# A two-block network on one core: the first inverse level, a value tile, a table product and a norm's order are moved, and unread products are added

## The reference, cut to what matters

```python
def stick_breaking_attention(u, w_q, k, v, w_o):
    q = (u @ w_q)... * (SB_HEAD_DIM ** -0.5)
    z = jnp.einsum("bhqd,bhkd->bhqk", qi, kj)
    lo = jnp.where(valid, jax.nn.log_sigmoid(-z), 0.0)
    ...
    o = o + jnp.einsum("bhqk,bhkd->bhqd", jnp.exp(logw), vj)

def second_block(x, ...):
    mod = (c_act @ w_mod[l] + b_mod[l])[:, None, :]
    sh1, sc1, g1, sh2, sc2, g2 = jnp.split(mod, N_MOD, axis=-1)
    h = rms_norm(x, norm1_w[l]) * (1.0 + sc1) + sh1
    x = x + g1 * token_mixer(h, rel_bias, w_in[l], ...)
    ...

def gated_delta_rule(q, k, v, beta, g):
    ...
    kb = k * beta[..., None]
    A = jnp.eye(C) + jnp.where(strict, jnp.einsum('bhnid,bhnjd->bhnij', kb, k) * dec, 0.0)
    u = lax.linalg.triangular_solve(A, v * beta[..., None], unit_diagonal=True)
    w = lax.linalg.triangular_solve(A, kb * jnp.exp(G)[..., None], unit_diagonal=True)
    ...
```

## Time and profile before

| what | value |
|---|---|
| runs | 1360.14 us median of 3 (1359.49 to 1363.82) |
| profiled execution | 1361.18 us, of which 1359.3 are the span of the profile |
| mean granted TensorE clock | 0.987 of full speed |
| TensorE busy | 1309.9 us, 96% |
| VectorE busy | 991.8 us, 73% |
| ScalarE busy | 722.1 us, 53% |
| GpSimd busy | 130.5 us, 10% |
| DMA | 289.77 MB, mean 213 GB/s |

### The profile page before, as it was taken

How to read it: one execution, slowest core, us unless ns; L and a number is a source line. 1 busy time by engine, 2 the same in 40 slices (tenths; PEclk the granted TensorE clock), 3 DMA queues, 4 the chain that set the end, 5 groups by cost and what they waited for, 6 DMA issues and landing times.

```text
span 1359.3 us, 18977 instructions
## 1 busy us (share of the span) xinstructions
PE 1309.9 (96%) x8008; PEld 1147.5 (84%) x8008; DVE 991.8 (73%) x1135; ACT 722.1 (53%) x768; POOL 130.5 (10%) x118
## 2 busy tenths in 40 slices
PE   7999999999999999999999899999999999999996
PEld 7999888899998798799999688798887888888884
DVE  6978566677878735857865755747566889989886
ACT  6665773244443546544444364717324667776763
POOL 0002543200001000000000100026100000000000
PEclk9999999999999999999999899999999999999999
DMA  8543225377878442357765354321345689999992
GB/s 332 180 172 124 94 94 193 145 283 282 308 279 311 182 155 94 124 204 282 284 253 187 124 186 156 139 94 32 124 155 202 221 336 372 335 350 337 352 357 94
DMA packets 41625, 289.77 MB, mean 213 GB/s; under 512 B 4637, under 2 KB 5045, under 8 KB 7488
## 3 DMA queue, kind: packets, MB, share of 16 engines
q1 hardware_dynamic: 35712, 252.76, 50.4%
q0 software_dynamic: 5824, 35.74, 7.0%
HBM read 286.38 MB, written 2.11 MB: 212 GB/s over the span
## 4 chain that ended last, share of the span: by engine, by line
PE 80%; DVE 13%; ACT 3%; issue 2%; DMA 1%; POOL 1%; DVEq 0%; SPq 0%; ACTq 0%; POOLq 0%
PE banks L851 23%; PE banks L853 22%; PE banks L852 22%; DVE w_lo L1649 3%; PE banks L1412 2%; ACT w_hi L398 1%; PE banks L1515 1%; DVE conv L1695 1%; DVE qkvT L2026 1%; DVE mod L1892 1%; DVE pre_norm L1807 1%; PE banks L1194 1%; DMA raw<-weights 1%; PE banks L1026 1%; POOL tiny L2429 1%
## 5 line engine op out<-in xcount | busy, mean ns | idle before, releaser
L1649 DVE TENSOR_TENSOR w_lo<-raw,w_hi 128x2048 fp32r<-128x2048 f32 x237 | 542.4, 2295 | 111.5 <-ACT w_hi L398 110.1
L398 ACT ACTIVATE w_hi<-raw 128x2048 fp32r<-128x2048 f32 x237 | 450.6, 1910 | 24.3 <-DMA raw<-weights 24.1
L851 PE MATMUL banks<-hT_hi,w_hi 128*128 128x256 f32 x1120 | 320.9, 287 | 3.0 <-DVE w_lo L1680 3.0
L853 PE MATMUL banks<-hT_hi,w_lo 128*128 128x256 f32 x1120 | 318.0, 284 | 0.0
L852 PE MATMUL banks<-hT_lo,w_hi 128*128 128x256 f32 x1120 | 317.9, 284 | 0.0
L851 PEld LDWEIGHTS banks<-hT_hi,w_hi 128*128 128x128 f32 x1120 | 215.9, 193 | 8.9 <-issue 6.0
L852 PEld LDWEIGHTS banks<-hT_lo,w_hi 128*128 128x128 f32 x1120 | 216.0, 193 | 1.1
L853 PEld LDWEIGHTS banks<-hT_hi,w_lo 128*128 128x128 f32 x1120 | 215.8, 193 | 0.0
L851 PE MATMUL banks<-w_hi,act_hi 128*128 128x512 f32 x256 | 100.1, 391 | 0.4 <-DVE act_lo L1863 0.4
L852 PE MATMUL banks<-w_lo,act_hi 128*128 128x512 f32 x256 | 99.9, 390 | 0.0
L853 PE MATMUL banks<-w_hi,act_lo 128*128 128x512 f32 x256 | 99.6, 389 | 0.0
(11 more groups left out here) (425 smaller groups left out, 2119.8 us busy)
## 6 DMA issues: line engine op xcount, KB each, us to landing
raw<-weights SPq DMA_DIRECT2D x238, 1024.0 KB, 4.9
mod_raw<-weights POOLq DMA_DIRECT2D x24, 1024.0 KB, 5.2
ln_gain_bias<-ln_rows POOLq DMA_DIRECT2D x4, 1024.0 KB, 8.2
h<-x SPq DMA_DIRECT2D x2, 512.0 KB, 4.2
h<-x POOLq DMA_DIRECT2D x1, 1024.0 KB, 5.4
rms_gain<-rms_rows POOLq DMA_DIRECT2D x2, 512.0 KB, 6.5
h_rows<-h POOLq DMA_DIRECT2D x1, 1024.0 KB, 4.5
bias_rows<-bias_table POOLq DMA_DIRECT2D x1, 1024.0 KB, 9.0
```

The costliest lines, as they stand in the source:

```text
L398: A(hi[u % RING][:, :], raw[u % RING][:, :], ACT.Copy).then_inc(S["w_hi_done"], 1)
L851: mm(out, a[0], b[0], start=start, stop=False)
L853: return mm(out, a[1], b[0], start=False, stop=stop)
L1649: tt(lo[u % RING][:, :], raw[u % RING][:, :], hi[u % RING][:, :].bitcast(F32), ALU.subtract).then_inc(S["w_lo_done"], 1)
```

## The change

It does six things.

1. `v_tile(2, 0)` goes ahead of `sb_scores(0)`. On VectorE `mod_part(14)` goes ahead of the two value splits, and the split of the key unit behind the two constants.
2. TensorE issues eleven products of 512 columns (`unread`), after a wait for the seventh `ln_var`. They multiply the old `hT_hi` with itself into bank 4, and nobody reads them; the transposes overwrite the bank.
3. `ln_sum` can do one half alone. For the second tile's sum in the norm the two halves stand around `rms_shift(0, 0)`, and `tile_low(4, 0, 4)` comes ahead of `ln_stats(1)`.
4. The bias table's product goes ahead of the tiles of the second row tile, into bank 0, with its three waits. Its copy on VectorE goes from behind the delta rule's decay to right behind `tile_low(4, 1, 4)`. TensorE waits for that copy before it writes bank 0 again.
5. The system times beta is written to `Ub`, and TensorE transposes `Ub`.
6. The two `Xi` operations of both tiles are done from `Ub` before the wait for the transposed system; only the two `XiT` operations of each tile stay behind it.

```diff
+            def unread(b, n):
+                for _ in range(n):
+                    mm(PS[:, b, :], hTh[:, 0, 0:P], hTh[:, 0:2, :].rearrange("p k t -> p (k t)"), start=True, stop=True)
...
+            v_tile(2, 0)
             sb_scores(0)
-            v_tile(2, 0)
             v_tile(2, 1).then_inc(S["unit_done"], 1)
...
+            pe.wait_ge(S["ln_var"], 7)
+            unread(4, 11)
             to_T_tile(4, 0, hn0, 14, 4)
             for n in range(3):
                 va_zb_tile(n, 0)
             to_T_tile(4, 1, hn0, 16, 4)
+            pe.wait_ge(S["tab_in"], 32)
+            pe.wait_ge(S["pool_init"], 2 + 1)
+            pe.wait_ge(S["mod_read"], 12)
+            mm(PS[0:H_A, 0, 0:TABLE_W], relb[:, :], tabs[:, 0:TABLE_W], start=True, stop=True
+               ).then_inc(S["small_mm"], 1)
             for n in range(3):
                 va_zb_tile(n, 1).then_inc(S["unit_done"], 1)
...
-            pe.wait_ge(S["tab_in"], 32)
-            pe.wait_ge(S["pool_init"], 2 + 1)
-            mm(PS[0:H_A, 5, 0:TABLE_W], relb[:, :], tabs[:, 0:TABLE_W], start=True, stop=True
-               ).then_inc(S["small_mm"], 1)
-            pe.wait_ge(S["mod_read"], 12)
+            pe.wait_ge(S["tab_sb"], 1)
             for n in range(4):
                 unit_T(at(("qa", "ka")[n // 2], n % 2), hT, [PS[:, n, c * T:(c + 1) * T] for c in range(2)])
...
-                    last = pe.transpose(tr_bank(0, 2 + t)[:, n, :], Xi[:, 4 * t + n, :], ident)
+                    last = pe.transpose(tr_bank(0, 2 + t)[:, n, :], Ub[:, 4 * t + n, :], ident)
...
-            def ln_sum(r, t, last_unit, banks):
+            def ln_sum(r, t, last_unit, banks, parts=(0, 1)):
...
-                for c, s in halves():
+                for c, s in halves()[parts[0]:parts[-1] + 1]:
...
+            mod_part(14)
             plain_splits("v", 2)
-            mod_part(14)
-            split(at("k") + AHEAD)
             mod_part(15)
             dve.tensor_copy(ident_r[:, :], ident).then_inc(S["sb_const"], 1)
             ts(past_r[:, :], before, -1.0, -NEG, ALU.add, ALU.mult).then_inc(S["sb_const"], 1)
+            split(at("k") + AHEAD)
             split(at("q") + AHEAD)
...
-            ln_sum(3, 1, at("va"), 4)
+            ln_sum(3, 1, at("va"), 4, (0,))
             rms_shift(0, 0)
+            ln_sum(3, 1, at("va"), 4, (1,))
+            tile_low(4, 0, 4)
             ln_stats(1)
-            tile_low(4, 0, 4)
...
             tile_low(4, 1, 4)
+            dve.wait_ge(S["small_mm"], 2 + 1)
+            dve.tensor_copy(tabs[0:H_A, TABLE_W:2 * TABLE_W - 1], PS[0:H_A, 0, 0:TABLE_W - 1][:, ::-1]
+                            ).then_inc(S["tab_sb"], 1)
             plain_splits("mlp1", 1, 31)
...
-            dve.wait_ge(S["small_mm"], 2 + 1)
-            dve.tensor_copy(tabs[0:H_A, TABLE_W:2 * TABLE_W - 1], PS[0:H_A, 5, 0:TABLE_W - 1][:, ::-1]
-                            ).then_inc(S["tab_sb"], 1)
...
-                tt(Xi[:, 4 * t:4 * t + 4, :], tr_bank(0, (1, 4)[t]), per(beta[:, 4 * t:4 * t + 4]), ALU.mult
+                tt(Ub[:, 4 * t:4 * t + 4, :], tr_bank(0, (1, 4)[t]), per(beta[:, 4 * t:4 * t + 4]), ALU.mult
                    ).then_inc(S["m_read"], 1)
...
+            dve.wait_ge(S["m_read"], TT)
+            for t in range(TT):
+                b = slice(4 * t, 4 * t + 4)
+                step(tt(Xi[:, b, :], Ub[:, b, :], wide(lev[:, 7, :]), ALU.mult))
+                step(tt(Xi[:, b, :], wide(ident), Xi[:, b, :], ALU.subtract))
             for t in range(TT):
                 dve.wait_ge(S["n_read"], t + 1)
                 b = slice(4 * t, 4 * t + 4)
                 step(tt(XiT[:, b, :], NT[:, b, :], wide(lev[:, 0, :]), ALU.mult))
-                step(tt(XiT[:, b, :], wide(ident), XiT[:, b, :], ALU.subtract))
-                step(tt(Xi[:, b, :], Xi[:, b, :], wide(lev[:, 7, :]), ALU.mult))
-                tt(Xi[:, b, :], wide(ident), Xi[:, b, :], ALU.subtract).then_inc(S["x_upd"], 1)
+                tt(XiT[:, b, :], wide(ident), XiT[:, b, :], ALU.subtract).then_inc(S["x_upd"], 1)
```

## The result

The changed kernel takes **1351.97 us** median of 5 runs (1350.95 to 1355.23) against 1361.67 of the kernel before in the same comparison (5 runs, 1359.49 to 1363.82): ratio 0.9925, 95% interval 0.9907 to 0.9942, so 9.7 us faster by the medians and 10.2 by the ratio. Forecast were 1350.0 and a gain of 10.1. The forecast started from the median of three runs, 1360.14; with five the kernel before is at 1361.67, so 1.5 of the 2.0 us between 1350.0 and 1351.97 are the base and not the gain.

The account below looks back on a forecast made before the run. TensorE's own instructions were taken as the bound, four fifths of the chain of waits, VectorE 13%. Terms 1.7 + 3.3 + 0.7 + 4.4 = 10.1 us brought the median from 1360.14 to 1350.0; range 1346.6 to 1354.0.

Parts of the forecast that it names:

- Value tile: First stick-breaking scores: value tile ahead of them removes TensorE's waits for qT and mask; 1.7 us, bounds 0.7 and 1.9.
- the mask must be too: First scores: the mask must be ready early as well; VectorE's new order brings it 5 us earlier, at 466.5.
- Order of the norm: Second block's first norm: VectorE's new order brings the first product 1.35 us earlier, the transposes 0.55 earlier.
- Clock of the norm: Second block's first norm: eleven unread products hold the clock, so 36 products take 8.3 instead of 10.22; 1.9 us.
- Norm together: Second block's first norm: new order and held clock together gain 3.3 us; bounds 0.9 and 3.4.
- Table: Table product moves off TensorE's path into idle time behind the second transposes; 0.7 us, bounds 0 and 0.74.
- Delta rule: Inverse's first level: 2.8 us from the second tile's earlier product, 1.7 from the clock; 4.4 in all, bounds 1.5 and 4.5.
- the clock falls in the norm all the same: Rival, chance 0.20: norm's clock drops despite unread products, only the order helps; 0.9 instead of 3.3, time 1352.4.
- The delta rule's lower bound: Rival, chance 0.09: inverse's second tile still late and clock still drops; gain 1.5, time 1352.9.
- The last stage takes it back: Rival, chance 0.06: weight stream sets the experts' pace, earlier gains are waited away; within 4 us of 1360.
- Slower by the bias transfer: Rival, chance 0.03: bias transfer, moved to 780, holds up a needed weight; 3.8 us slower, 1363.9.
- other low stretches: After 800, low-clock stretches may come or go as work moves, 1.7 us each; two gone gives 1346.6.

Follow-up runs that it names:

- undo_mask: Changed kernel with only VectorE's old order around the mask restored, the mask behind the k split again; median 1353.11 us.
- undo_order: Changed kernel with VectorE's old order in the norm restored and the unread products kept; median 1353.00 us.
- undo_unread: Changed kernel without the eleven unread products, the norm's new order kept; median 1353.04 us.
- undo_table: Changed kernel with the bias table's product and copy back in their old places; median 1354.26 us of eleven runs.
- full: The changed kernel as it is, run and profiled again as base of the follow-up experiments; median 1351.66 us.
- undo_delta: Changed kernel with the first level of the delta rule's inverse as before; median 1357.22 us.
- hold2: Changed kernel plus seven unread products before block attention's first transposes, gate tile halved around the one-column sums, new norm order in the first block's layer norms; median 1349.35 us.

## Why the prediction was right, step by step

The total was right (a gain of 10.2 by the ratio for 10.1), and so were its parts, with one false reason.

- **Value tile, 1.7**: 1.70 by S to H. The step behind it that failed is "the mask must be too" early: what the text prices at 5 us of VectorE's time is worth nothing (undo_mask). The forecast put the mask's need where TensorE waited for it before. There it asked at 471.82 - 0.95 = 470.87; in undo_mask it asks at 473.98, in a profile whose S is 1.2 later, so the need moved back by 1.9 us with the scores, and the old 0.95 is covered. Only the reason was false, not the sum.
- **Order of the norm**: the first product 1.35 earlier was forecast; from M it is 8.83 against 10.08, so 1.25, and the transposes 0.50 earlier for 0.55.
- **Clock of the norm, 1.9**: undo_order holds the unread products alone and reaches the second transposes 1.90 earlier than before (18.40 from M against 20.30).
- **Norm together, 3.3**: 3.17, from M to the second transposes (17.13 against 20.30). Order alone gives 20.30 - 19.48 = 0.82 (undo_unread), the lower bound of 0.9 in the text. The two alone, 0.82 and 1.90, add up to 2.72; the other 0.45 comes only with both, since without the unread products the transposes run at the lower level (1.97 instead of 1.32) and use up part of what the order wins.
- **Table, 0.7**: 0.79 by undo_table. GpSimd's transfer of the bias rows takes 10.0 instead of 9.0 at its new place, and no wait for a weight follows.
- **Delta rule, 4.4**: 4.14. The term that was mis-sized is the set of four products: 0.9 in the text, 3.86 / 4 = 0.965 measured, which makes the gain 0.26 smaller. The stall of 2.59 and its clock went as forecast. VectorE's two operations beside GpSimd took 1.67 each, and its four early ones stepped by 0.72.

Of the rivals, **the clock falls in the norm all the same** is refuted in its place: the window from 767.67 has 1.00, and all eleven profiles with the eleven products are like it. Without the unread products it falls (undo_unread), with four of them it falls for half as long, with eleven it holds even over 2.65 us of idle time around the transposes (undo_order). The Trainium skill ("TensorE: Matmul & The Clock Gate", Part 4: PE-mode transpose) says that a transpose doesn't count as a busy TensorE the way a product does. By that rule the norm would have given 0.9; it gave 3.17. No run here shows what a transpose counts, since products stand on either side of each round. **The delta rule's lower bound** is refuted by 3.86. **The last stage takes it back**: from the gather's products to the end it is 306.4 before, 306.0 after and 305.9 in full, so it takes nothing. **Slower by the bias transfer**: no wait came of it.

What the forecast lacked is the scatter. It let other low stretches come or go at 1.7 us each, and this was the right size: the profile of after has two at double length, full has not. But it took them for a consequence of moved work. They also move from execution to execution of the same work, and such dips, not the change, make the profile of after 3.4 us longer than that of full. The chance of 0.62 was for a sum whose scatter the forecast hadn't measured: that the total came within 0.4 us of it is closer than medians of five can promise, and in that part luck.

## What to carry over

Where a profile shows a stall followed by a low clock, price both, and look at whether filling the stall with unread products is cheaper than shortening it: here eleven products cost nothing and held 1.9 us, four gave only part. Where the clock falls with no stall ahead, look for a run of very narrow products: making them wide cost 0.1 us, and the dip was in neither of two profiles. Price a part by distances between instructions in two traces, where these repeat to 0.06 us, and use the runs for the total only. Before one profile is taken as proof that a dip is gone, count in how many profiles without the edit it was there: ten of ten at 881, nine of eleven at 830. A part under 2 us could not be seen in medians of five or six runs that scatter by 3 to 9.

## What was unexpected

- **Up to 128 columns width is all but free for unrounded products.** Records of one column and records of 128 columns both start 0.112 us apart at the full clock; most of the difference between 3.73 and 3.84 for 32 lies in the first step (0.13 and 0.21).
- **The low clock doesn't need idle time.** Full has it at 881.5 with TensorE busy 3.40 of 3.40 us, behind one-column sums. At 1024.9 it is there too, behind the router's products of 36 columns, which follow each other without a gap. That these are its cause is not shown; they weren't tried with more columns.
- **The same code meets the dips in different places.** Up to S nothing differs between after, full and undo_delta, and they reach it at 441.0, 440.8 and 443.9 us.
- **A dip's length isn't fixed either**: in the same kernel 3.4 and 3.4 in full, 6.8 and 6.8 in after at the same two places; with other code there 10.2 in hold2 at the second.
